# Cached page keys transposed on VectorE in 32x32 blocks instead of on TensorE, inside the attention of a two-layer decoder step

## What is computed

```python
ckv_past = cache_ckv[j, page_table].reshape(Bs, past_len, KV_LORA)      # 8, 4096, 256
kr_past = cache_krope[j, page_table].reshape(Bs, past_len, ROPE_D)      # 8, 4096, 64
def mla_sample_attend(q_lat, q_rope, ckv_new, kr_new, ckv_past, kr_past):
    s_past = latent_scores(q_lat, q_rope, ckv_past, kr_past)   # 8 heads: q_lat.ckv + q_rope.kr, scaled
    s_new = latent_scores(q_lat, q_rope, ckv_new, kr_new)
    p = softmax(concatenate([s_past, s_new]))
    return p[past] @ ckv_past + p[new] @ ckv_new               # the context, 8 heads x 256 channels
```

## Time and profile before

| what | value |
|---|---|
| device time, three executions | 2794.82 us median (2793.02, 2794.82, 2804.56) |
| profiled execution, first to last instruction | 2804.0 us |
| TensorE busy | 2691.9 us, 96% of the span |
| VectorE busy | 1723.8 us, 61% |
| ScalarE busy | 1111.5 us, 40% |
| GpSimd busy | 1239.7 us, 44% |
| mean granted TensorE clock | 0.987 of full |
| chain that ended last | TensorE 72%, VectorE 14%, issue 4%, ScalarE 3% |

### The profile page before, as it was taken

One profiled execution on the slowest core, in us unless ns is written; L12 is line 12 of the kernel. 1 busy time (PEld: TensorE's weight loads), 2 busy tenths in 40 slices (PEclk: granted clock), 3 DMA queues, 4 the chain that ended last, 5 costly groups with the idle time before them and its releaser, 6 DMA issues.

```text
span 2804.0 us, 61530 instructions
## 1 busy us (share of the span) xinstructions
PE 2691.9 (96%) x21801; PEld 2491.0 (89%) x21801; DVE 1723.8 (61%) x3199; ACT 1111.5 (40%) x2499; POOL 1239.7 (44%) x1296
## 2 busy tenths in 40 slices
PE   6999999998999999999899999999998999999998
PEld 5898999998999999999887787878788999999998
DVE  4677678665333336896546666666675434358984
ACT  5121212354444445442543333333364444444444
POOL 3000000455555566544753333333376666665544
PEclk8999999999999999999999999999999999999999
DMA  7422111635666754743133434343453343547442
GB/s 258 144 77 91 48 46 38 208 125 155 204 202 205 213 180 151 260 167 95 54 111 110 148 105 143 105 145 118 147 176 96 118 145 117 150 155 253 165 144 105
DMA packets 385187, 397.91 MB, mean 142 GB/s; under 512 B 27587, under 2 KB 346678, under 8 KB 383046
## 3 DMA queue, kind: packets, MB, share of 16 engines
q1 hardware_dynamic: 362994, 363.57, 41.0%
q10 hardware_dynamic: 13780, 23.05, 2.3%
q0 software_dynamic: 8192, 8.40, 1.0%
HBM read 291.46 MB, written 103.48 MB: 141 GB/s over the span
## 4 chain that ended last, share of the span: by engine, by line
PE 72%; DVE 14%; issue 4%; ACT 3%; POOL 2%; SPq 2%; DMA 2%; DVEq 0%; ACTq 0%; POOLq 0%
PE bank L4068 18%; PE bank L4069 18%; PE bank L4070 17%; PE bank L4691 3%; PE bank L4811 2%; PE bank L4705 2%; DVE xT L3552 1%; DVE stage L3523 1%; DVE td L3529 1%; DVE xT L3545 1%; PE bank L4197 1%; PE bank L4732 1%; POOL op_l L1407 1%; PE bank L4359 1%; PE bank L4797 1%
## 5 line engine op out<-in xcount | busy, mean ns | idle before, releaser
L1407 POOL TENSOR_TENSOR op_l<-raw,op_h 128x512 fp32r<-128x512 f32 (+1 forms) x396 | 518.7, 1314 | 419.8 <-ACT op_h L2076 405.4
L4068 PE MATMUL bank<-t_high,op_h 128*128 128x258 f32 x1736 | 497.7, 287 | 15.2 <-ACT tq L2104 7.5
L4069 PE MATMUL bank<-t_low,op_h 128*128 128x258 f32 x1736 | 493.3, 284 | 0.0
L4070 PE MATMUL bank<-t_high,op_l 128*128 128x258 f32 x1736 | 490.7, 283 | 0.0
L4068 PE MATMUL bank<-hh,whi 128*128 128x344 f32 (+3 forms) x1324 | 436.5, 330 | 20.1 <-POOL hl L1302 4.3
L4070 PE MATMUL bank<-hh,wlo 128*128 128x344 f32 (+3 forms) x1324 | 419.9, 317 | 0.0
L4069 PE MATMUL bank<-hl,whi 128*128 128x344 f32 (+3 forms) x1324 | 419.4, 317 | 0.0
L4068 PEld LDWEIGHTS bank<-t_high,op_h 128*128 128x128 f32 x1736 | 329.2, 190 | 29.1 <-issue 23.4
L4069 PEld LDWEIGHTS bank<-t_low,op_h 128*128 128x128 f32 x1736 | 331.0, 191 | 0.0
L4070 PEld LDWEIGHTS bank<-t_high,op_l 128*128 128x128 f32 x1736 | 330.5, 190 | 0.0
L4068 PE MATMUL bank<-td,op_h 128*128 128x258 f32 x1008 | 289.2, 287 | 18.4 <-DVE xT L3552 15.1
(11 more groups left out here) (521 smaller groups left out, 6241.4 us busy)
## 6 DMA issues: line engine op xcount, KB each, us to landing
raw<-in_w_gu SPq DMA_DIRECT2D x84, 512.0 KB, 4.6
pk<-in_cache_ckv SPq DMA_DIRECT2D x256, 128.0 KB, 2.4
ada_x<-in_w_ada SPq DMA_DIRECT2D x28, 1024.0 KB, 8.4
act_high<-st_all SPq DMA_DIRECT2D x86, 258.0 KB, 5.3
act_low<-st_all SPq DMA_DIRECT2D x86, 258.0 KB, 5.2
act_raw<-tq SPq DMA_DIRECT2D x164, 129.0 KB, 4.0
raw<-in_w_down SPq DMA_DIRECT2D x48, 384.0 KB, 4.3
wst<-in_w_in_even SPq DMA_DIRECT2D x28, 512.0 KB
```

Of the source, the lines that this page charges most:

```text
L1407: nc.gpsimd.tensor_tensor(op_l[p][:, 0:t.half, :], op_source(p, t), op_h[p][:, 0:t.half, :].bitcast(F), ALU.subtract).then_inc(op_lo.sem, 1)
L4068: mm(out, wh_, xh_, start=start, stop=False, skip_group_check=more)
L4069: mm(out, wh_, xl_, start=False, stop=False, skip_group_check=more)
L4070: return mm(out, wl_, xh_, start=False, stop=stop, skip_group_check=more)
```

## The change

The page keys are no longer turned by TensorE. VectorE transposes blocks of 32x32 directly from `pk` to `keyb` (two instructions of 128x1024 a step, `keys_out`) and from `pr` (two of 128x256, `ropes_out`). Such a transpose exchanges tokens and channels only within a block, so afterwards each quarter of the partitions holds the channels of another 32 tokens. The queries are made to fit: `queries_repeated` has SP copy each pair of samples' queries into all quarters (24 DMAs within SBUF a round), and `query_blocks` on VectorE spreads them over four column blocks with a mask (`blk`), so that the stationary operand is block-diagonal, 128x32. `page_scores` then takes 10 blocks of channels (8 latent, 2 rotary) by 4 groups: 40 matmuls with 32 stationary and 64 moving columns. The scores fill all 128 rows of bank 6, with 64 columns. ScalarE's exponential writes every probability four times, VectorE masks the turned probabilities with `blk` in place of copying a part of them, and `page_values` has 32 stationary columns in place of 8. Totals and weights are reduced over four times as many rows (`block_masks`, `weights_of`, `shares`). The bank 5 list has only the probabilities and the three ends of a round. ScalarE no longer copies keys. SP issues `queries_repeated(0)` before page step 1, and `queries_repeated(r + 1)` in step 4 of round r, behind page step 6.

```diff
-FILLS = []
-for _d in range(STEPS):
-    FILLS += [("ropes", _d), ("keys", _d, 0)] + ([("probs", _d - 1)] if _d > 0 else []) + [("keys", _d, f) for f in (1, 2, 3)]
-FILLS += [("probs", STEPS - 1), ("peaks",), ("weights",), ("sums",)]
+FILLS = [("probs", _d) for _d in range(STEPS)] + [("peaks",), ("weights",), ("sums",)]
...
+GB = P // CG
+KB = CT * P // GB
+RB = ROPE // GB
+QB = KB + RB
+NEWS = 2 * GB
...
+            def queries_repeated(r):
+
+                if r > 0:
+                    sp.wait_ge(q_ready, 3 * r)
+                for i in range(CG):
+                    rows = slice(i * GB, (i + 1) * GB)
+                    for jj in range(P // GB):
+                        sp.dma_start(qrep[rows, CT * jj:CT * jj + CT], qall[jj * GB:(jj + 1) * GB, 0:CT, 2 * r:2 * r + 2, :]
+                                     ).then_inc(qrep_in.sem, 16)
+                    for jj in range(RB):
+                        sp.dma_start(qrep[rows, KB + jj], qall[jj * GB:(jj + 1) * GB, CT, 2 * r:2 * r + 2, :]).then_inc(qrep_in.sem, 16)
...
                 sp.wait_ge(knew_ready, 1)
+                queries_repeated(0)
                 tokens_saved()
                 page_step(0, 1)
...
                             page_step(r, d + 2)
+                        if r < PAIRS - 1 and d == 4:
+                            queries_repeated(r + 1)
...
                     if s >= 2:
-                        pool.wait_ge(fill_ready, (s - 2) // STEPS * NF + FILL["ropes", (s - 2) % STEPS] + 1)
+                        pool.wait_ge(*key_ready(ropes_turned(s - 2)))
...
+                else:
+                    pool.wait_ge(ds_ready, PAIRS * (CG * STEPS) + 1)
...
-                    nc.scalar.activation(pd[:, 0:w], bank[6][:, 0:w], ACT.Exp, bias=negm[:, d:d + 1], scale=MLA_SCALE,
+                    else:
+                        nc.scalar.activation(pd[:, 2 * P:2 * P + NS], bank[6][:, NEWS:NEWS + NS], ACT.Exp, bias=negm[:, d:d + 1],
+                                             scale=MLA_SCALE, accum_out=drop[:, d:d + 1])
+                    nc.scalar.activation(pd[:, 0:2 * P].rearrange("p (a i b) -> p i a b", a=2, i=CG),
+                                         bank[6][:, 0:NEWS].rearrange("p (a b) -> p a b", a=2).unsqueeze(1).to_broadcast([P, CG, 2, GB]),
+                                         ACT.Exp, bias=negm[:, d:d + 1], scale=MLA_SCALE,
...
                 for d in range(STEPS):
                     u = 2 * d
-                    ropes_out(d)
                     probs(u + 1)
...
-                    keys_out(d, 1)
                     if u + 2 < 2 * TB:
                         probs(u + 2)
                     output(u)
-                    keys_out(d, 3)
...
+            def query_blocks(r, n):
+
+                if n == 0:
+                    dve.wait_ge(*qrep_in(16 * CG * (P // GB + RB) * (r + 1)))
+                on = blk[:].unsqueeze(1).unsqueeze(3)
+                for dst, first, end in ((qbd_r[:], KB, QB), (qbd_k, 0, KB)):
+                    ins = v.tensor_tensor(dst, qrep[:, first:end, n, :].unsqueeze(2).to_broadcast([P, end - first, CG, MH]),
+                                          on.to_broadcast([P, end - first, CG, MH]), ALU.mult)
+                ins.then_inc(q_ready, 1)
...
-            def keys_out(r, d, f):
-                dve.wait_ge(fill_ready, r * NF + FILL["keys", d, f] + 1)
+            def ropes_out(r, d):
+
                 dve.wait_ge(ds_ready, r * (CG * STEPS) + CG * d + 1)
-                v.tensor_copy(keyt[f // 2][:, f % 2 * 4:f % 2 * 4 + 4, :], bank[5].rearrange("p (j m) -> p j m", m=P)
-                              ).then_inc(fill_out, 1)
+                for half in range(2):
+                    dve.wait_ge(rope_in[2 * (d % 2) + half], 64 * (r * (STEPS // 2) + d // 2 + 1))
+                    v.transpose(keyrt[:, half], pr[2 * (d % 2) + half][:].rearrange("p g c -> p (g c)")).then_inc(key_ready.sem, 1)
+
+            def keys_out(r, d, half):
+                dve.wait_ge(page_in[2 * (d % 2) + half], 16 + 64 * (r * (STEPS // 2) + d // 2 + 1))
+                v.transpose(keyt[half], pk[2 * (d % 2) + half][:].rearrange("p g c -> p (g c)")).then_inc(key_ready.sem, 1)
...
-                    order.put(v.tensor_copy(ptd[:], turned))
-                    ins = v.tensor_copy(ptn[:], bank[5][0:NS, 2 * P:2 * P + MH])
-                else:
-                    ins = v.tensor_copy(ptd[:], turned)
-                ins.then_inc(fill_out, 1)
+                    order.put(v.tensor_copy(ptn[:], bank[5][0:NS, 2 * P:2 * P + MH]))
+                v.tensor_tensor(ptd[:].rearrange("p a (g i h) -> p (a g) i h", g=CG, i=CG),
+                                bank[5][:, 0:2 * P].rearrange("p (a i h) -> p a i h", i=CG, h=MH),
+                                blk[:].unsqueeze(1).unsqueeze(3).to_broadcast([P, 2 * CG, CG, MH]), ALU.mult).then_inc(fill_out, 1)
...
                     turned(u)
-                    keys_out(r, d, 0)
+                    if d % 4 == 0:
+                        query_blocks(r, d // 4)
+                    ropes_out(r, d)
...
                     if u + 2 < 2 * TB:
                         maxima(u + 2)
+                    keys_out(r, d, 0)
                     if d > 0:
                         page_sums(r, d - 1)
                     turned(u + 1)
-                    keys_out(r, d, 2)
+                    keys_out(r, d, 1)
                     low_output(u)
...
             def page_scores(r, d):
 
                 n = d // 4
-                filled(r, "keys", d, 3)
+                pe.wait_ge(*key_ready(keys_turned(r * STEPS + d)))
                 pe.wait_ge(da_ready, r * STEPS + d + 1)
-                if d == 0:
-                    pe.wait_ge(q_ready, r + 1)
-                for part_ in range(CT + 1):
+                if d % 4 == 0:
+                    pe.wait_ge(q_ready, 3 * r + 2 + n)
+                for j in range(QB):
                     for g in range(CG):
-                        q = q2[:, part_ if part_ < CT else CT + g % 2, n, :]
-                        k = keyb[:, :, (2 * g + part_) * P:(2 * g + part_ + 1) * P] if part_ < CT else keyr2[:, :, g // 2, :]
-                        ins = mm(bank[6][g * GC:g * GC + MH, 0:2 * P], q, k, start=part_ == 0, stop=part_ == CT)
+                        if j < KB:
+                            at = g * CT * P + key_block(j) * GB
+                            k = keyb[:, :, at:at + GB]
+                        else:
+                            at = g * ROPE + (j - KB) * GB
+                            k = keyrt[:, :, at:at + GB]
+                        ins = mm(bank[6][g * GC:(g + 1) * GC, 0:NEWS].rearrange("p (a b) -> p a b", a=2),
+                                 (qbd_k[:, j] if j < KB else qbd_r[:, j - KB]).rearrange("p i h -> p (i h)"), k, start=j == 0, stop=j == QB - 1)
...
-                        out = bank[6][g * GC:g * GC + MH, 2 * P:4 * P]
-                        mm(out, ptd[:, half * CG + g, :], pk[2 * (d % 2) + half][:, g, :], start=half == 0, stop=half == 1
+                        out = bank[6][g * GC:(g + 1) * GC, 2 * P:4 * P]
+                        mm(out, ptd[:, half, g * GC:(g + 1) * GC], pk[2 * (d % 2) + half][:, g, :], start=half == 0, stop=half == 1
...
                     if d > 0:
                         page_scores(r, d - 1)
-                    ropes(r, d)
                     turned(u)
-                    keys(r, d, 0)
...
-                    keys(r, d, 1)
                     turned(u + 1)
-                    weighed(u, lambda: keys(r, d, 2))
-                    keys(r, d, 3)
+                    weighed(u)
```

More of the change, by code:

```diff
@@ L490, in trunk @@
         last_sq[5] = [rs, sw[0], sw[1]]
+        os_at = used["keep"]
         os32 = lay("keep", "os32", [P, MH, NS])
@@ L572, in trunk @@
         keyb = nc.alloc_sbuf_tensor_at("keyb", [P, 2, KT * N], F, offset=w_at - KT * N * 4 - N * 4)[:, :, 0:TB * P]
-        keyt = [keyb[:, b].rearrange("p (j m) -> p j m", m=P) for b in range(2)]
-        keyr2 = keyr.rearrange("p (b a) m -> p b a m", b=2)
+        keyt = [keyb[:, b] for b in range(2)]
+        keyrt = keyr.rearrange("p k m -> p (k m)").rearrange("p (b x) -> p b x", b=2)
         free_h, free_l = (nc.alloc_sbuf_tensor_at(f"free{b}", [P, (KT - O0) * N], F, offset=w_at - b * KT * N * 4 - (KT - O0) * N * 4)
@@ L3709, in queries, with block_masks @@
                 v.tensor_copy(q2[:], qall[:, :, bass.ds(2 * r, 2), :]).then_inc(q_ready, 1)
+            def query_blocks(r, n):
[6 more added lines that the diff above has]
+                ins.then_inc(q_ready, 1)
+            def block_masks():
+                order.put(v.tensor_reduce(blk[:], ident[:].rearrange("p (i b) -> p i b", i=CG), axis=AX.X, op=ALU.add))
+                order(v.tensor_reduce(selh[:], ident[:].rearrange("p (q h) -> p h q", h=MH), axis=AX.X, op=ALU.add))
             def sample_queries():
@@ L3758, in page_maxima @@
                     w += NS
-                    new = bank[6][:, 2 * P:w]
+                    new = bank[6][:, NEWS:w]
```

(24 more changed lines are left out.)

48 lines of the change are left out of this document (26 added, 22 removed).

## The result

The changed kernel takes 2822.79 us (median of 13 executions, 2808.93 to 2826.97) against 2800.18 us for the kernel before (13 executions, 2791.41 to 2811.3). The ratio is 1.0071, with a 95% interval of 1.0056 to 1.0086: slower by 0.7%. The forecast was 2785, a gain of 10 us; the measured time lies inside the range and on the wrong side of no change.

A forecast was written before the change was run, and what follows sets the result against it. TensorE was taken to set the pace before, and a loop through TensorE and VectorE after. Terms: -26.7 + 9.1 + 4.8 + 2 = -10.8 us; rounded to 10 off 2794.8, this gave 2785, range 2757 to 2826.

The forecast's parts named there:

- So 24 take 10.3 us (8 to 13): SP's queue: issuing a round's 24 query copies at 0.43 us each takes 10.3 us, bounds 8 to 13.
- What it costs on SP: Forecast section on SP's query copies: 9.1 us in round 0, 4.8 at later page loads, 2 for TensorE's clock.
- The 0.43: Assumed issue time in us of one query copy on SP, from SP's nearest pairs; bounds 0.34 and 0.55.
- Round 0: VectorE waits at query_blocks for the first 24 copies, delaying the first page scores; cost 9.1 us.
- Page load 7: Step 4 of rounds 0 to 2: copies ahead of this load make VectorE wait in step 7; 1.6 us each, 4.8 total.
- 1 us in round 0 and up to 3 in the others: Stated sensitivity: how far the forecast sum moves for each 0.04 us by which a copy's issue differs from 0.43.
- The clock after the waits: TensorE's granted clock falls behind round 0's wait of 9 us; cost 2 us.
- The step: 10.7 forecast: One attention page step through VectorE and TensorE falls from 11.2 to 10.7 us; four rounds gain 26.7.
- a loop through both engines: Attention step: both key transposes stand between a maximum and the page scores, so neither engine alone sets the 10.7 us.
- Fast and slow transposes: Rivals on VectorE's 1024-element transposes: 0.75 us each gives 2758, chance 0.10; 2.3 us each gives 2845, chance 0.10.
- The narrow matmuls: Rival: page-score records have a 25 ns floor, so page scores take 2.0 us; total 2802, no change; chance 0.12.
- The clock's fall in every step: Rival: 1.5 us of TensorE idle beside narrow scores lowers its clock every step; +48 us, 2833; chance 0.12.

The follow-up runs named there:

- e3: The kernel before with only the 24 query copies a round added on SP's queue, their result unused: 2855.91 us, ratio 1.019 to the kernel before.
- e4: The changed kernel with the 24 query copies a round made by ScalarE, none issued by SP: 2767.14 us, ratio 0.9868 to the kernel before.
- e6: The kernel with ScalarE's copies, each key transpose on VectorE done twice: 2908.73 us, ratio 1.038 to the kernel before.
- e5: The kernel with ScalarE's copies, VectorE's first key transpose put ahead of the masked probabilities: 2750.30 us, ratio 0.9813 to the kernel before.

## Why the prediction was wrong

**The step that failed** is the term "So 24 take 10.3 us (8 to 13)" of "What it costs on SP". It measured 16.3 to 17.1 us, beyond its upper bound of 13. The 0.43 came from two stores to device memory, 0.45 us apart, the nearest rows that the trace of before had; the copies are SBUF to SBUF, and no row of before was one. e3 shows the cost without the rest of the change (+53.3 us), e4 the rest without the cost (-35.5, 2767.14 less 2802.60).

**Round 0: 9.1 forecast, 13.6 measured** against the kernel before by the clock of the trace, 14.9 counted from the second unit's scores. VectorE was at the wait at 1504.6, not 1506.0; the copies landed at 1520.2, not 1515.8. The walk behind it was right: from there to the first page scores 6.1 us forecast, 6.11 measured (1520.16 to 1526.27).

**Page load 7: 1.6 a round forecast, 9.74 to 11.0 of VectorE's wait measured.** In round 1 the pieces from the page scores of step 4 (1717.95) on are: load 6 done after 10.1 (9.9 forecast), copies 17.1 (10.3), table reads 4.6 (4.4), issues and landing 4.7 (4.3). So the pages were used at 1754.4, 36.4 us on, for 28.9. VectorE wanted them after 25.4, for 27.1, since the steps were shorter than forecast. Of the 9.4 us missed, 6.8 are the copies, the rest the walk. The forecast's remark that each 0.04 of an issue moves the sum by "1 us in round 0 and up to 3 in the others" gives +6 in round 0 for the 0.68 us an issue measured there and some +20 in the others for 0.70 to 0.71, and so a sum of about +15 in place of -10.8; measured was +20.6. The one term turns the gain into a loss by the forecast's own working.

**The clock after the waits: 2 us forecast for round 0 only.** It fell behind all four waits. Behind round 0's it was 0.50 until 1525.6, which costs TensorE's work from 1521.8 on about 2 us, as priced. The three last steps grew by 33.8 us where VectorE waited 30.5, and the stretches between rounds by 4.4 over e4; the forecast had nothing for these.

**The step: 10.7 forecast, 10.0 to 10.5 measured; right in kind.** The loop's terms against the rows above, forecast first: transpose 1 to page scores 1.33, 1.29; page scores 1.30, 1.26; turning the unit 0.93, 0.74; next scores 1.84, 1.83; probabilities turned and seen 0.42, 0.42; masked 0.43, 0.34; scaling and low half 0.81, 0.66; maximum 1.39, 1.39; transpose 0 1.15, 1.16; sums 0.63, 0.60; copy 0.44, 0.34. Sum 10.67 and 10.03. Two terms (0.93, 0.81) were read from the same step of the kernel before, and the same work on blocks of the same size now follows closer (turning the unit 0.74, scaling and low half 0.66); the runs do not show why. The copy and the multiply were taken 0.1 too long. The two steps with the new token took 10.53 and 10.23 where 11.20 was forecast. In e4, six steps gained 8.8 us in rounds 1 and 2 (7.7 in round 0, 6.2 in round 3) where 4.85 was forecast, the last step 0.6 where 1.6 was. Together the four rounds gained 33.8 us for 26.7. So the gain side was under-estimated while its mechanism, a loop through both engines, was right; that the measured time still lies inside the stated range owes something to this error, which worked against the other: without the extra 7.1 us of gain it would be 2829.9, above 2826.

**The rivals.** Fast and slow transposes are both out: 1.234 us for 1024 elements, and 421 ns for 256 (from the same groups), which is (1234 - 421) / 768 = 1.06 ns an element. The Trainium skill, "Vector Engine (DVE) Microarchitecture Reference", section 3.8, has one element per cycle per lane; the trace agrees, as these took what a tensor-tensor of that length does. The narrow matmuls are out too: 80 records in 1.26 us, 1697.81 to 1699.07. The Trainium skill, "TensorEngine Tiling (Array Packing)", Performance Considerations, would make them about 2.0 us, an estimate from its 60 cycles a matmul with each record counted as one; the measurement decides, and a pass of four records in different column groups cost about 1.26 / 20 = 0.06 us. The clock's fall in every step did not come with idle times of 1.4 to 1.8 us: it came in single steps (one in e4's 28), and in all 28 of e6 with some 4 us. So that rival had a mechanism that exists, and a frequency that these idle times did not give. The forecast had no rival for the copies beyond the stall that it priced; the mechanism on the slower side that it named, slow transposes, was not the one that decided.

## What to carry to other kernels

A layout change that frees a compute engine must be priced at the queue that prepares its operands: 96 DMAs of 2 to 4 KB cost this kernel more (53 us, e3) than moving the key transposes to VectorE gained it (35 us, e4), because everything behind them in an in-order queue waits too. Look for an engine with free time for small rearrangements within SBUF (here 0.2 us each on ScalarE, for 0.64 on SP's queue). And a term that no row of its own kind prices needs a wide upper bound where an engine's whole order waits behind it. After moving work between two engines, walk the loop through both and take one piece out of it: the reorder in e5 took 0.2 to 1.1 us off each of the steps 1 to 6.

## What the runs showed of the hardware

- The issue of a DMA on SP's queue took 0.60 us (0.64 from start to start) for SBUF to SBUF, whether to 32 or 128 partitions, and 0.47 from start to start for the same destinations from device memory; before, two stores to device memory were 0.45 apart. Among the 24 of a batch a few were longer, so that batches took 0.68 to 0.71 an issue.
- With idle times of 0.5 to 1.8 us ahead of the page scores in a 10 us step, TensorE's clock stayed at 2.4 GHz in 27 of e4's 28 steps and fell to 1.2 GHz for about 3 us in one; with 3.1 to 4.5 us in a 14 us step (e6) it fell in all 28 and came back within the step.
- Four f32 records of 64 columns in four column groups cost about 0.06 us together, also with a new stationary operand for each, so that 40 products of that width took less time than 12 of 256 columns had (1.26 us for 1.41).
